# Six dummy products between the up products of a batch's two pairs, from the eleventh batch on

## The reference

```python
def one_block(args):
    toks, e = args
    xb = x_pad[toks]                                  # the rows that chose expert e
    hb = jax.nn.silu(xb @ w1[e]) * (xb @ w3[e])       # 1024 -> 256, gate and up
    return hb @ w2[e]                                 # 256 -> 1024, down
y = jax.ops.segment_sum(y_rows * row_gate[:, None], row_tok, num_segments=T + 1)[:T]
```

## Time and profile before

| | us |
|---|---|
| median of 3 runs | 1150.2 |
| lowest, highest | 1149.04, 1150.66 |
| the profiled execution | 1149.34 |
| its span, from the first to the last instruction | 1147.5 |
| TensorE products busy | 1044.8 (91% of the span) |
| VectorE, ScalarE busy | 403.6, 260.5 |
| moved by DMA | 441.05 MB, mean 384 GB/s |

### The profile page before, as it was taken

The page is one execution under the profiler, slowest core; times in us unless marked ns, Lnnn a source line. Parts: engine busy times, 40 slices in busy tenths (PEclk is TensorE's granted clock), DMA queues, the critical chain, the costliest instruction groups (busy, mean ns, idle before and its releaser), DMA issues.

```text
span 1147.5 us, 26693 instructions
## 1 busy us (share of the span) xinstructions
PE 1044.8 (91%) x11382; PEld 534.4 (47%) x11382; DVE 403.6 (35%) x1189; ACT 260.5 (23%) x683; POOL 18.7 (2%) x36
## 2 busy tenths in 40 slices
PE   9999999898899898888899999989889999988888
PEld 5665753344444343333466657434444344333333
DVE  4865532223222222221268656322322222222213
ACT  1245321111221111111131544121221111111111
POOL 0010000000000000000000100000000000000000
PEclk9999999999999999999999999999999999999999
DMA  9967699999999999999996677999999999999997
GB/s 310 335 241 293 260 398 428 427 426 426 428 430 428 427 428 429 428 428 422 384 310 220 267 297 280 410 419 425 426 426 429 428 428 428 430 428 428 428 421 272
DMA packets 72861, 441.05 MB, mean 384 GB/s; under 512 B 16480, under 2 KB 36064, under 8 KB 43616
## 3 DMA queue, kind: packets, MB, share of 16 engines
q1 hardware_dynamic: 72512, 439.52, 93.6%
q0 software_dynamic: 144, 0.58, 0.1%
q10 hardware_dynamic: 144, 0.07, 0.0%
HBM read 439.10 MB, written 1.05 MB: 384 GB/s over the span
## 4 chain that ended last, share of the span: by engine, by line
PE 83%; DVE 7%; DMA 5%; issue 3%; SPq 1%; ACT 1%; another core or an unknown queue 0%; POOL 0%; DVEq 0%
PE bank L1172 15%; PE bank L1087 15%; PE bank L1184 10%; PE bank L693 8%; PE bank L1069 8%; PE bank L1102 4%; DMA w_odd<-in_moe_w 4%; PE bank L819 4%; PE bank L1137 3%; PE bank L1056 2%; DVE moe L1750 2%; PE bank L1178 2%; DVE moe L1713 1%; PE bank L963 1%; DMA w_even<-in_w_in 1%
## 5 line engine op out<-in xcount | busy, mean ns | idle before, releaser
L1811 ACT ACTIVATE moe<-bank 128x512 f32<-128x512 f32 (+2 forms) x164 | 84.2, 523 | 560.8 <-PE bank L1087 278.8
L1713 DVE COPY moe<-bank 128x512 f32<-128x512 f32 x64 | 44.3, 692 | 321.2 <-PE bank L1087 260.2
L1184 PE MATMUL bank<-moe 128*128 128x512 f32 (+1 forms) x264 | 121.2, 601 | 25.8 <-DVE moe L1750 24.7
L1172 PE MATMUL bank<-w_even,moe 64*32 64x512 f32 x896 | 99.0, 590 | 10.2 <-DVE moe L1734 10.2
L1087 PE MATMUL bank<-w_odd,moe 64*32 64x512 f32 x1536 | 90.9, 619 | 12.2 <-issue 6.1
L1069 PE MATMUL bank<-moe,x 128*64 128x64 f32 x3072 | 98.0, 224 | 1.3 <-issue 1.3
L1069 PEld LDWEIGHTS bank<-moe,x 128*64 128x64 f32 x3072 | 94.6, 138 | 5.4 <-issue 5.4
L1087 PE MATMUL bank<-w_even,moe 64*32 64x512 f32 x1536 | 88.0, 601 | 8.1 <-issue 8.1
L1184 PEld LDWEIGHTS bank<-moe 128*128 128x128 f32 x264 | 47.8, 192 | 99.8 <-DVE moe L1750 51.4
L1172 PE MATMUL bank<-w_odd,moe 64*32 64x512 f32 x768 | 84.8, 590 | 7.5 <-DVE moe L1734 7.5
L1750 DVE COPY moe<-bank 128x512 f32<-128x512 f32 x32 | 22.1, 692 | 197.2 <-PE bank L1172 178.0
(11 more groups left out here) (203 smaller groups left out, 1010.8 us busy)
## 6 DMA issues: line engine op xcount, KB each, us to landing
w_even<-in_moe_w SPq DMA_DIRECT2D x76, 2048.0 KB, 37.0
w_odd<-in_moe_w SPq DMA_DIRECT2D x72, 2048.0 KB, 35.3
w_odd<-in_moe_w SPq DMA_DIRECT2D x44, 1024.0 KB, 10.3
w_even<-in_moe_w SPq DMA_DIRECT2D x40, 1024.0 KB, 9.8
w_even<-in_w_in SPq DMA_DIRECT2D x24, 768.0 KB, 11.5
w_odd<-in_w_out SPq DMA_DIRECT2D x4, 2048.0 KB, 12.9
w_odd<-in_moe_w SPq DMA_DIRECT2D x8, 512.0 KB, 11.1
w_even<-in_w_in SPq DMA_DIRECT2D x4, 416.0 KB, 6.8
```

What stands on the lines that cost most here:

```text
L1172: last = mm(bank[h][BLK * k:BLK * (k + 1), :], hT_pair[rows, c, BLK * q:BLK * (q + 1)], w2_pairs[parity][q][rows, c, 512 * h:512 * h + 512 ...
L1184: return mm(Y[t][h][:, lo - 512 * h:hi - 512 * h], scatter[:, t * P:(t + 1) * P], y_rows[:, lo:hi], start=False, stop=True, skip_group_che ...
L1713: nc.vector.tensor_copy(partial[:, k, :], source[:, :]).then_inc(part_dve.sem, 1)
L1811: return fn(dst, src, ACT.Copy)
```

## The change

`batch` gets a parameter `warm`; where it is set, that many dummies into bank 2 are placed after the products of pair 0 and before those of pair 1, that is, before the wait for pair 1's up loads. The loop over the batches is split in two: the first runs batches 4 to 9 as before, the second batches 10 to 13 with `warm=6`, and batch 14, behind the loops, has it too. `BATCHES` is 16.

```diff
-                def batch(j, parity, seen=None, pairs=True, next_pairs=True):
+                def batch(j, parity, seen=None, pairs=True, next_pairs=True, warm=0):
                     b = b0 + (j + parity)
                     pe.wait_ge(xg_dve.sem, b + 1)
                     if seen is None:
                         for q in range(NB // 2):
+                            if q and warm:
+                                keep_warm(warm, bank[2])
                             up_gate_pair(j, parity, q)
...
-                with pe.Fori(4, m, 2) as j:
+                with pe.Fori(4, BATCHES - 6, 2) as j:
                     batch(j, 0)
                     batch(j, 1)
-                batch(m, 0, next_pairs=False)
+                with pe.Fori(BATCHES - 6, m, 2) as j:
+                    batch(j, 0, warm=6)
+                    batch(j, 1, warm=6)
+                batch(m, 0, next_pairs=False, warm=6)
                 last_batch(m)
```

## The result

The changed kernel takes 1152.5 us (median of 20 runs, 1151.12 to 1156.51) against 1150.2 us before (20 runs); the ratio is 1.0026, 95% interval 1.0018 to 1.0033. That is slower by some 3.0 us (2.1 to 3.8), where I had forecast 1151.1 us and no change that can be told. The ratio is estimated from the runs of both kernels; the two medians alone differ by 2.3 us, which its interval holds. The time lies inside the range I gave, near its upper end; the direction was missed.

The account below looks back on a forecast made before the run. The weight stream was taken as the bound in late batches. From 1149.34 us, -1.70 for the clock and +1.5 a layer for the blocks gave 1150.6; half of 0.86 made it 1151.1 us, range 1148.0 to 1152.8.

Parts of the forecast that it names:

- What bounds the kernel: Late batches, from batch 11 on: the weight stream is the bound, 88.08 us for three batches, and TensorE waits.
- What the dummies cost: Before the second pair's wait: six dummies take 1.45 us, free in pauses of about 3 us, exposed time taken by the next.
- What the second loop costs: Batches 10 and 11: reading the new body's 6.0 instruction blocks a layer makes the weight stream 1.5 us later in each layer.
- The estimate by bytes: Second loop's block reading: six blocks of 0.0163 MB at 429 GB/s would cost the weight stream 0.23 us.
- What the clock gives back: Batch 14's second pair: no longer slow, saving 1.70 us in the first layer and nothing in the second.
- the sum: Whole kernel: first layer -0.2 us, second +1.5, together +1.3 on the profiled 1149.34 us, giving 1150.6 before the median allowance.
- The half of 0.86 us: Whole kernel: half the median's distance above the profiled execution, added in case it is one more slow batch 14.
- the hidden blocks: Rival, second loop: the six blocks fall on DMA engines that have time, the stream stays as it was; 1148.1 us, chance 0.17.
- A body that isn't kept: Rival, jump from batch 11 to 12: six blocks read again in both layers, another 1.5 us a layer; 1154.1 us, chance 0.07.
- The clock that falls all the same: Rival, one batch 14: the remaining 1.6 us of idling still bring 1.2 GHz, +1.7 us; 1152.8 us, chance 0.10.

## Why the prediction missed

**What bounds the kernel**: right. The weight stream decides the start of batch 14's second pair, and TensorE most of what follows: time added there counts, as the run with late dummies shows.

**What the dummies cost**: right for this change. 1.54 us each batch where I had 1.45, in pauses or made up by the next one. The condition that I named, that the cover must be there, is what the run with dummies in every batch lost.

**What the second loop costs**: right, to the term. Six blocks a layer, in batches 10 and 11, kept afterwards; 1.5 us a layer, measured 1.5 and 1.5. It rested on a comparison of two stretches of one trace, one with blocks and one without. The estimate by bytes, 0.23 us, was a sixth of it. The Trainium skill's page DMA: Bandwidth & Descriptors, section Queues, rings and completion order, says that a DMA engine serves the queues with work for it in turn, packet by packet. The trace agrees with that as far as it goes: a block kept an engine for 1.1 us on average (six blocks in 0.6% of sixteen engines' 70 us), and the spread of the landings grew by 1.5 us. That the turns are the reason is argued, not shown. Nothing was read between 470 and 520 us, after the second loop's jump back, so the new body was kept like the first. The rule that I weighed from the Trainium skill's page Runtime: NRT & Kernel Launch, section Instruction fetch mechanics, a new read at a taken branch out of its window, is again not what the trace shows.

**What the clock gives back**: this step failed. I credited -1.70 us in the first layer, because batch 14 was slow in the one execution I had. Dummies in batch 14 alone, which were to give that credit and nothing else, gave 0.9999: a gain of 0.1 us, with ends of -1.0 and +1.4. With a credit near 0 the sum reads 0 + 1.5 + 1.5 = +3.0 us, which is the ratio of 1.0026. (From the median of 1150.2 that makes 1153.2 us; 1152.5 were measured. The half of 0.86 us that I added for the distance to the median was a guess.)

Why the credit is so small is shown in part. First, one execution stood for all: three traces have no, one and two slow pairs in batch 14. But three of six is as many as I credited, so this alone doesn't make it 0, and an account by turns, slow pairs in 11 and 13 and none in 14, fits only one trace of the three in both layers. Second, I wrote that after batch 14 no arrival stops TensorE, and had read it off the last two down loads in a layer whose pair was slow. With a fast pair TensorE comes 1.7 us earlier and can meet earlier loads of the last batch: it waited 0.44 us for the third down load in the first layer of the second trace of the kernel before, and 1.09 us in all in the second layer of the run with dummies in batch 14 alone, where 0.3 us of the 1.7 were left. (Of the six down loads the first two are of 1 MB and four of 0.5 MB.) How much of the credit each of the two takes in an average execution stays open.

**The rivals**: the hidden blocks are excluded by three runs that lay the loop out again, in ratio and in arrivals. A body that isn't kept did not occur. The clock that falls all the same occurred once in the trace of the changed kernel, in batch 12, and the pauses behind it took it up before batch 14.

## What to carry to other kernels

Code that is laid out again is not free where the weight stream is the bound: here the blocks of one more body, some 1500 TensorE instructions, put some DMA engines back, and that cost 1.5 us a layer that nothing made up. Before a gain is read from one trace, ask whether the event it removes is there in each execution, and look again at every wait behind it with the gain already taken: what had room beside a slow pair may not have it beside a fast one. Filling half of a pause held the clock here in all places but one, but a slow pair that is followed by another pause costs nothing, and there is then nothing to win.

## What the runs showed of the hardware

A pause of about 3 us doesn't decide the clock by its length: after 3.04 (rows 2) and 3.11 us the pair ran at 3.67 us, after 2.99 and 3.05 us at 5.4. No pair in these traces was slow after a pause of 1.86 us or less, and one was after 1.6 us of dummies and 2.64 us of idling. A slow pair of 5.37 us ran in part at 1.2 GHz (granted clock 0.68), pairs of 3.67 us at 2.4 (1.00 in the changed kernel's batches 11 and 14). Reading six blocks of 16 KB, 0.10 MB in all, made a saturated stream 1.5 us later, whether they were read in batches 6 and 7 or 10 and 11, and twelve blocks 3.0 us (in the kernel with three loops, the spread between first and last engine grew from 3.8 to 6.9 us in the first layer).
